# Attention values of a fused two-block kernel: high and low parts of the values side by side in one stationary tile, and a summing step of its own

## The reference

```python
SWA_Q_HEADS, SWA_KV_HEADS, SWA_HEAD_DIM, WINDOW, BLOCK = 16, 2, 64, 128, 128

def swa_attention(q, k, v, sinks):        # q (1,512,16,64), k and v (1,512,2,64)
    # a block of 128 queries sees its own block of keys and the one before it
    scores = jnp.einsum('bnqhgd,bnkhd->bnhgqk', qb, kk) * 64 ** -0.5
    scores = jnp.where(valid, scores + alibi, NEG)
    probs = jax.nn.softmax(jnp.concatenate([scores, sink], axis=-1), axis=-1)[..., :-1]
    return jnp.einsum('bnhgqk,bnkhd->bnqhgd', probs, vv)

for l in range(2):                        # first block
    h = rmsnorm(x, attn_norm_g[l]); proj = h @ w_in[l]
    ya = swa_attention(qa, ka, va, swa_sinks[l]) * jax.nn.silu(ga)
    yb = mla_attention(...) * jax.nn.silu(gb)
    x = x + jnp.concatenate([ya, yb], axis=-1) @ w_out[l]
```

## Time and profile before

| what | value |
|---|---|
| median of 3 runs | 2791.2 us (2790.09 to 2793.32) |
| profiled execution: its own time | 2790.87 us |
| profiled execution: span | 2789.1 us |
| granted clock of TensorE, mean | 0.994 |
| HBM traffic | 103 GB/s over the span |

### The profile page before, as it was taken

The page is one execution under the profiler, slowest core; times in us unless marked ns, Lnnn a source line. Parts: engine busy times, 40 slices in busy tenths (PEclk is TensorE's granted clock), DMA queues, the critical chain, the costliest instruction groups (busy, mean ns, idle before and its releaser), DMA issues.

```text
span 2789.1 us, 33326 instructions
## 1 busy us (share of the span) xinstructions
PE 2732.7 (98%) x13100; PEld 2271.2 (81%) x13100; DVE 1241.8 (45%) x1831; ACT 1000.0 (36%) x1566; POOL 1089.6 (39%) x544
## 2 busy tenths in 40 slices
PE   8999998999999999899999999999999999999997
PEld 7888887888888888788878888888878888888886
DVE  6466636622346663672335545553443222222223
ACT  5244435523223443553433333332223323332222
POOL 1443332344443433334443333334344444444442
PEclk9999999999999999999999999999999999999998
DMA  6432231254443223124442232222223333336333
GB/s 183 132 84 76 73 121 45 66 142 143 123 132 91 69 76 121 45 67 138 138 120 76 76 83 76 73 80 80 87 83 121 113 109 111 114 113 211 117 125 113
DMA packets 307611, 289.13 MB, mean 104 GB/s; under 512 B 33152, under 2 KB 256000, under 8 KB 306944
## 3 DMA queue, kind: packets, MB, share of 16 engines
q1 hardware_dynamic: 300512, 264.40, 32.0%
q10 hardware_dynamic: 6944, 22.61, 2.1%
HBM read 260.19 MB, written 26.74 MB: 103 GB/s over the span
## 4 chain that ended last, share of the span: by engine, by line
PE 84%; DVE 11%; DMA 2%; ACT 1%; issue 1%; POOL 0%; SPq 0%; DVEq 0%; ACTq 0%
PE bank L873 25%; PE bank L875 24%; PE bank L874 24%; PE work L1131 1%; DMA w_raw<-in_w_in 1%; DVE pt L1728 1%; PE o_bank L874 1%; PE o_bank L875 1%; DVE mixed L1475 1%; PE work L987 1%; PE work L989 1%; PE o_bank L873 1%; DMA latent_scr<-mixed 1%; DVE probs L1680 1%; DVE mixed L1471 1%
## 5 line engine op out<-in xcount | busy, mean ns | idle before, releaser
L850 POOL TENSOR_TENSOR w_lo<-w_raw,w_hi 128x1024 fp32r<-128x1024 f32 (+3 forms) x460 | 982.0, 2137 | 1367.5 <-ACT w_hi L699 1367.5
L873 PE MATMUL bank<-act_in,w_hi 128*128 128x512 f32 x2662 | 1054.0, 396 | 12.8 <-DVE act_in L1443 9.9
L875 PE MATMUL bank<-act_in,w_lo 128*128 128x512 f32 x2662 | 1041.0, 391 | 0.0
L874 PE MATMUL bank<-act_in,w_hi 128*128 128x512 f32 x2662 | 1039.7, 391 | 0.0
L699 ACT ACTIVATE w_hi<-w_raw 128x1024 fp32r<-128x1024 f32 (+3 forms) x468 | 438.0, 937 | 1049.3 <-PE bank L875 648.4
L873 PEld LDWEIGHTS bank<-act_in,w_hi 128*128 128x128 f32 x2662 | 501.0, 188 | 116.8 <-DVE act_in L1443 11.2
L875 PEld LDWEIGHTS bank<-act_in,w_lo 128*128 128x128 f32 x2662 | 500.5, 188 | 107.2
L874 PEld LDWEIGHTS bank<-act_in,w_hi 128*128 128x128 f32 x2662 | 501.2, 188 | 98.9 <-issue 1.7
L873 PE MATMUL bank<-mixed,w_hi 128*128 128x512 f32 x768 | 299.7, 390 | 0.0
L875 PE MATMUL bank<-mixed,w_lo 128*128 128x512 f32 x768 | 299.1, 389 | 0.0
L874 PE MATMUL bank<-mixed,w_hi 128*128 128x512 f32 x768 | 299.0, 389 | 0.0
(11 more groups left out here) (267 smaller groups left out, 2703.7 us busy)
## 6 DMA issues: line engine op xcount, KB each, us to landing
w_raw<-in_w_in SPq DMA_DIRECT2D x512, 128.0 KB, 2.5
w_raw<-in_w_in SPq DMA_DIRECT2D x224, 256.0 KB, 2.9
w_raw<-in_w_out SPq DMA_DIRECT2D x64, 512.0 KB, 3.7
w_raw<-in_w_in SPq DMA_DIRECT2D x32, 512.0 KB, 3.7
w_raw<-in_w_out SPq DMA_DIRECT2D x64, 256.0 KB, 4.6
x_scr<-buf ACTq DMA_DIRECT2D x32, 256.0 KB, 3.2
probs<-x_scr SPq DMA_DIRECT2D x32, 256.0 KB, 5.0
w_raw<-in_w_attn_up SPq DMA_DIRECT2D x32, 256.0 KB, 2.9
```

What stands on the lines that cost most here:

```text
L850: nc.gpsimd.tensor_tensor(lo, raw, hi, ALU.subtract).then_inc(lo_ready, 1)
L873: pe.matmul(dst, lhs[0], rhs[0], start=start, stop=False, skip_group_check=skip)
L874: pe.matmul(dst, lhs[0], rhs[1], start=False, stop=False, skip_group_check=skip)
L875: return pe.matmul(dst, lhs[1], rhs[0], start=False, stop=stop, skip_group_check=skip)
```

## The change

In `plan_steps` each SWA head gets a further step, `swa_sum`, five slots behind its transposes (three slots behind its values), and three slots behind them (one behind the values) for k = 3. The zeros go: `v_swa` now holds, for each key block and head, 64 high columns and 64 low columns side by side. A block's values are two matmuls: high and low columns together by the high data, all 128 output rows, then the 64 high columns by the low data, into rows 0 to 63. At the end rows 0 to 63 hold two of the three products and rows 64 to 127 the third. In `swa_sum` ACT copies rows 64 to 127 to `swa_lo` (the buffer `sq`), and DVE adds rows 0 to 63 into the head's half of `swa_sum` (the buffer `acc2`); for e = 1 it then multiplies by the gate and splits as before. Each head now raises `y_done` and each head's values wait for it, since a bank holds one head. `swa_values`, once a layer, writes the new layout with two instructions instead of five.

```diff
-                                                       (turn + 2, "values")])
+                                                       (turn + 2, "values"), (turn + (3 if k == 3 else 5), "swa_sum")])
@@
-        ys += 0 if h["kind"] == "swa" and h["e"] == 0 else 1
+        ys += 1
@@
-        v_swa = y_flat[:, 0:1536].rearrange("p (s b c) -> p s b c", s=2, b=NB)
+        v_swa = y_flat[:, 0:1024].rearrange("p (b e s c) -> p b e s c", b=NB, e=2, s=2)
+        swa_lo, swa_sum = sq, acc2
@@ scalar
+                elif name == "swa_sum":
+                    act.wait_ge(pv_done, step[1] + 1)
+                    act.activation(swa_lo[0:64, :], o_bank[64:128, :], ACT.Copy).then_inc(o_lo, 1)
@@ tensor, values
-                    if h["y0"] and h["e"] == 0:
+                    if h["y0"]:
                         pe.wait_ge(y_done, h["y0"])
@@
-                            v = v_swa[:, :, j, 64 * h["e"]:64 * h["e"] + 128]
+                            both = v_swa[:, j, h["e"], :, :].rearrange("p s c -> p (s c)")
+                            pe.matmul(o_bank[:, j * P:j * P + w], both, pt[:, 0, at:at + w],
+                                      start=j == 0, stop=j == NB - 1, skip_group_check=True)
+                            ins = pe.matmul(o_bank[0:64, j * P:j * P + w], both[:, 0:64], pt[:, 1, at:at + w],
+                                            start=False, stop=j == NB - 1, skip_group_check=True)
+                            continue
@@ vector, swa_values
-                    link(v.memset(v_swa[:, :, :, 64:128].bitcast(F32), 0.0))
                     src = work[1][:, :].rearrange("p (b a c) -> p b a c", b=NB, a=2)
-                    dst = v_swa.rearrange("p s b (a c) -> p s b a c", a=3)
-                    for e in range(2):
-                        link(v.tensor_copy(dst[:, 0, :, 2 * e, :], src[:, :, e, :]))
-                        link(v.tensor_tensor(dst[:, 1, :, 2 * e, :], src[:, :, e, :],
-                                             dst[:, 0, :, 2 * e, :].bitcast(F32), ALU.subtract))
+                    link(v.tensor_copy(v_swa[:, :, :, 0, :], src))
+                    link(v.tensor_tensor(v_swa[:, :, :, 1, :], src, v_swa[:, :, :, 0, :].bitcast(F32), ALU.subtract))
@@ vector, swa_sum
+                    if kind == "swa":
+                        v.wait_ge(o_lo, o_lo_before(h) + 1)
+                        own = head_rows(h["e"])
+                        ins = v.tensor_tensor(swa_sum[own, :], o_bank[0:64, :], swa_lo[0:64, :], ALU.add)
+                        if h["e"] == 1:
+                            link(ins)
+                            link(v.tensor_tensor(swa_sum[:, :], swa_sum[:, :], gate[:, t % 2, :], ALU.mult))
+                            link(split(y, swa_sum[:, :]))
+                            signal(y_done)
+                        else:
+                            ins.then_inc(y_done, 1)
                         continue
```

More of the change, by code:

```diff
@@ L423, in gate_views, with o_lo_before @@
             return [(gate[:, :, :], tmp[:, :, :])]
+        def o_lo_before(h):
+            return 16 * h["l"] + 2 * h["h"] + h["e"]
         def mix_gate(k):
@@ L443, in hybrid_program @@
         pv_done = sem("pv_done")
+        o_lo = sem("o_lo")
         y_done = sem("y_done")
@@ L1164, in _ @@
                                     (pt[:, 0, at:at + w], pt[:, 1, at:at + w]),
-                                    j == 0 and h["e"] == 0 and kind != "sb", j == NB - 1, skip=True)
+                                    j == 0 and kind != "sb", j == NB - 1, skip=True)
                     ins.then_inc(pv_done, 1)
@@ L1733, in _ @@
                                         ALU.subtract).then_inc(pt_lo, 1)
-                elif name == "output" or (name == "values" and heads[step[1]]["kind"] != "mla"):
+                elif name in ("output", "swa_sum") or (name == "values" and heads[step[1]]["kind"] == "sb"):
                     h = heads[step[1]]
                     kind, t = h["kind"], h["h"]
-                    if kind == "swa" and h["e"] == 0:
+                    y = mixed[:, 8 + t if kind == "mla" else t]
+                    if kind == "swa":
[9 more added lines that the diff above has]
+                            ins.then_inc(y_done, 1)
                         continue
                     v.wait_ge(pv_done, h["j"] + 1)
-                    y = mixed[:, 8 + t if kind == "mla" else t]
                     if kind == "mla":
@@ L1744, in _ @@
                         continue
-                    link(v.tensor_tensor(tmp[:, 0, :], o_bank[:, :], gate[:, t % 2 if kind == "swa" else 0, :],
-                                         ALU.mult))
+                    link(v.tensor_tensor(tmp[:, 0, :], o_bank[:, :], gate[:, 0, :], ALU.mult))
                     link(split(y, tmp[:, 0, :]))
```

## The result

| | before | after |
|---|---|---|
| median of the runs | 2792.1 us (7 runs, 2790.0 to 2793.3) | 2802.8 us (7 runs, 2798.6 to 2807.1) |
| ratio, 95% interval | | 1.0041 (1.0031 to 1.005) |
| profiled execution (span) | 2790.87 us (2789.1) | 2806.26 us (2804.5) |

The change makes the kernel 0.4% slower, by 10.7 us in the median. The predicted 2801.2 us is 1.6 us off. One of the eleven executions of experiment 2 took 3388.3 us at a mean granted clock of 0.75 and is left out of its ratio; every other one in this document lies within 0.2% of its kernel's median.

What follows compares the result with a forecast made beforehand. PE, busy for 98% of the span, was taken to bound the kernel. New waits of 24.8 us less 14.7 saved gave +10.1 us, so a median of 2801.2 us; the range was 2789 to 2806.

Steps and rivals of the forecast that it cites:

- part 1: PE's values of each SWA head: four of twelve matmuls go, saving 0.46 us a head, 14.7 us in all.
- The estimate by the Trainium skill: Weight load of the last, 128-column block of a head's values: about 0.05 us more saving a head, 1.6 us in all.
- part 2: DVE instructions with two SBUF inputs or fast casts and GpSimd instructions exclude each other; L1213 took 2.76 instead of 0.69 us.
- part 3: Third head of a group: PE waits 1.8 us before the fourth head's scores; 10.7 us, plus 3.4 in fourth groups.
- the first gap: Third head's row, between addition and multiplication: DVE's multiplication beats GpSimd by 0.03 us; otherwise the row ends 0.1 to 0.2 later.
- the same sum: Fourth group's third head, GpSimd in one double piece: part 3's reckoning, 0.1 us shorter, gives 1.7 us of wait, twice.
- part 4: End of a group: PE idles 1.2 us more at three joints per layer, 7.1 us; behind the fourth group 2.4 us.
- The sign that I gave: In the timeline, 1.2 to 1.4 us of idle time before the first transposes of groups two to four.
- part 5: First head of the fourth group: GpSimd wins against DVE's gate multiplication, PE's third scores wait 0.6 us, twice, 1.2 us.
- part 6: swa_values, once a layer: 0.9 to 1.0 us shorter, taken as 0 gain, and -2 at the low end.
- rival: Cases: as predicted 0.62, GpSimd in once 0.15, no holding 0.13, narrow products not overlapping 0.07, all else 0.03.
- the sum: Whole kernel: 24.8 us of new waits against 14.7 us saved, +10.1 us.

Runs made afterwards that it cites:

- experiment 2: The changed kernel, with GpSimd's low part of the chunk in the third head's row waiting until DVE's row is through; 2787.4 us, ratio 0.9983.
- Number 1: The kernel before with only the new values layout, two products per block and two-instruction swa_values, without copy and addition; 2777.2 us, ratio 0.9949.
- number 7: The changed kernel with swa_values written by five DVE instructions instead of two, in the new layout; one execution, 2800.1 us.
- 3: The changed kernel with all additions before the next head's norm and ACT's copy before its wait for the next head's scores; 2783.1 us, ratio 0.9968.
- number 5: Two kernels: changed kernel with additions and copy moved early, and the fourth head's split in the next group's slot 2 (2784.3 us) or slot 10 (2776.5 us).
- number 4: The changed kernel with all additions before the next head's norm, but ACT's copy left behind the next head's exponentials; 2863.9 us, ratio 1.0251.
- 5 (slot 2): The changed kernel with additions and copy moved early, and the fourth head's split in slot 2 of the next group; 2784.3 us, ratio 0.9974.
- 6: The kernel before with the new products, no copy or addition, and the second head's output behind the third head's norm; 2786.7 us, ratio 0.9977.

## Why the prediction was right, point by point

- **The removed products (part 1).** Right in kind, too small: from one head's transposes to the next the changed kernel takes 12.20 us instead of 12.76, so 0.56 a head and not 0.46. Products of 256 columns start 0.12 apart as before, but the two of the last block only 0.06 (234.90, 234.96, 235.02), with the 128-column load in it. I had read the pitch from 256-column products only. The estimate by the Trainium skill (TensorE: Matmul & The Clock Gate, LDWEIGHTS), 0.05 us more a head, pointed the right way and was half of it.
- **DVE and GpSimd (part 2).** Right, and shown by number 2: take GpSimd's pieces out of the row, and 15.4 us return.
- **The third head (part 3).** Predicted 1.8 us, idle time measured 1.80; even the order was right except that GpSimd won the first gap, by 0.09 us where I had given it to DVE by 0.03, at a cost that I had put at 0.1 to 0.2. PE lost 1.95. In the fourth group I said 1.7 and it was 1.14. The term that failed is "the same sum": in the other groups GpSimd also holds L1682 behind the third head's scores (0.91 us at 236.42; in the fourth group 0.23), so there the norm ends 0.7 us sooner before PE's transposes are due.
- **The end of a group (part 4).** From the fourth head's transposes to the next first transposes the changed kernel needs 0.71 us more (198.26 to 217.51, before 198.97 to 217.51); 0.72 was predicted. The sign that I gave, 1.2 to 1.4 us of idle time before the first transposes of groups two to four, failed as it stands: it was 0.96, 0.98 and 1.99 us, since 0.23 us of it fell earlier (208.08) and the fourth group had 0.98 us already before the change. Behind the fourth group PE waits 1.37 us, 1.2 predicted. Number 1 shows how much of a joint is the lost saving, 0.75 instead of 0.20 us without any addition.
- **The fourth group's first head (part 5).** GpSimd does win the race, but by less: 0.29 us of wait, 0.6 predicted.
- **`swa_values` (part 6).** 0 was right for the length of the step (number 7). The first layer gained 1.1 us there all the same, by a norm that starts 0.36 us sooner and is through its first instruction before GpSimd comes; the cause of that is open.
- **What was missing.** The clock: three falls to 1.2 GHz in this stage, some 4.7 us in the profiled execution, and 3.2 us in a fourth one behind it (1444.28). No rival had it, although the waits that bring it here were all predicted. The seven executions of the changed kernel scatter over 8.5 us, and their mean granted clock goes with the time (0.994 at 2798.6 us, 0.991 at 2806.2 to 2807.1). The kernel before does the same: its nineteen executions beside experiments 1 to 3 scatter over 7.5 us (0.995 at 2788.2, 0.992 at 2795.7). So the scatter is no trait of the change, and how much the clock adds to the median no run here shows.

The mechanism was right, and the closeness of the number was luck in part. The saving of each head was predicted 0.1 us short, and so was the time that PE loses at a long wait, by nearly 0.2 us. Without the four falls of the clock the traces add up to some 7.5 us (9.0 in the eight groups, less the 1.1 of the first layer and the 0.4), where the sum had 10.1. The falls, which the sum did not have, make 15.4 of it in the profiled execution. The medians, 10.7 us apart, lie between the two.

## What to carry to other kernels

A step that is added to an engine with idle time is paid by its place: ask which gap it fills, whether something else fills that gap already (number 5), and whether its own input comes before the gap or after (number 4). Where two engines exclude each other, every gap between two linked instructions is a place at which the other can come in; a row that has room for its own length may have none for two turns of the neighbour, and one wait on the neighbour gave back 15.4 us here, where moving the row gave 19.7 (numbers 2 and 3; the two together were not tried). And when a wait is new, count it from start to start (here the idle time and 0.27 us), and look at the granted clock behind it.

## What was not expected of the hardware

- During or behind a wait of PE the granted clock can fall to 1.2 GHz, and equal waits do not do equal things. In the SWA stage of the changed kernel and of experiments 2, 3, 5 (slot 2) and 7: of fifteen waits of 1.79 to 1.82 us one was followed by a fall (305.19), of ten of 1.95 to 2.01 us six, of the two longer ones (2.16 and 2.24) the first; shorter ones, at the joints and before scores, by none in this stage (1.75 us in the kernel before, 1.54 in number 1). In number 4 all eight of 4.3 to 4.6 us were (the clock was down before PE went on), and of six of 1.86 to 1.88 us two. Outside the stage even the wait of 1.14 us at 1444.28 was followed by a fall, and the same wait in the kernel before was not. What tells the equal ones apart stays open; it was not tried.
- GpSimd needs no more than the 0.03 us between two linked DVE instructions, and comes in at each such gap when it is due: in numbers 4 and 6 and in the changed kernel its two pieces took two turns each time. The Trainium skill (SBUF — State Buffer, Who interferes with whom) has the exclusion, and the 1.74, 1.40, 1.48 and 1.66 us agree with it; that the turn is lost in so short a gap is what the traces add. DVE's instructions with an input in PSUM kept their length beside it: L1745 of number 2 took 1.16 us for two at 241.18, next to GpSimd's piece at 241.17.
